# A mixture-of-experts stage whose record loads come in a fixed set per expert instead of one by one

## The reference, cut to what matters

```python
e_flat = expert.reshape(n_assign)            # 2048 tokens x top 2 = 4096 assignments, 32 experts
order = jnp.argsort(e_flat)
tok_sorted = order // TOP_K
...
def expert_block(args):
    xb, e = args
    return (jax.nn.silu(xb @ exp_w1[e]) * (xb @ exp_w3[e])) @ exp_w2[e]
...
y = y_buf.reshape(n_blocks * MOE_BLOCK, d)[dest] * gate_sorted[:, None]
out = jnp.zeros((n_tok, d), h.dtype).at[tok_sorted].add(y)
x = x + g2 * out
```

## Time and profile before

| | us |
|---|---|
| median of 3 runs | 2413.15 |
| the profiled execution, its own time | 2409.21 |
| its span, first to last instruction | 2407.5 |
| expert stage, within the span | about 1596 to 2406 |
| busy in the whole span: PE, DVE, ACT, POOL | 2227.6, 1430.2, 1181.7, 500.8 |
| mean granted TensorE clock | 0.970 |
| bytes moved by the hardware queue q1 | 354.24 MB, 44.6% of 16 engines' span |

### The profile page before, as it was taken

The page is one execution under the profiler, slowest core; times in us unless marked ns, Lnnn a source line. Parts: engine busy times, 40 slices in busy tenths (PEclk is TensorE's granted clock), DMA queues, the critical chain, the costliest instruction groups (busy, mean ns, idle before and its releaser), DMA issues. The chain is left out here.

```text
span 2407.5 us, 43378 instructions
## 1 busy us (share of the span) xinstructions
PE 2227.6 (93%) x15189; PEld 1549.2 (64%) x15190; DVE 1430.2 (59%) x2488; ACT 1181.7 (49%) x2106; POOL 500.8 (21%) x772
## 2 busy tenths in 40 slices
PE   5998999999979999789999999968899999999998
PEld 2335777888856666456666666746666776666775
DVE  4456686232325555555555555466677887666886
ACT  4556322222134444355555555345566666555674
POOL 2662111000001101001222222341222122222122
PEclk8999999999989999899999999979999999999999
DMA  8895222122374543522222221359897988887994
GB/s 303 279 272 139 62 53 79 56 85 62 78 207 98 124 100 89 171 54 80 73 74 71 62 80 58 130 181 330 299 317 254 371 308 290 287 257 252 325 330 145
DMA packets 242118, 414.31 MB, mean 172 GB/s; under 512 B 25601, under 2 KB 129365, under 8 KB 236915
## 3 DMA queue, kind: packets, MB, share of 16 engines
q1 hardware_dynamic: 198048, 354.24, 44.6%
q0 software_dynamic: 18800, 44.94, 7.6%
q10 hardware_dynamic: 25125, 13.18, 2.0%
HBM read 344.83 MB, written 76.85 MB: 175 GB/s over the span
## 5 line engine op out<-in xcount | busy, mean ns | idle before, releaser
L937 PE MATMUL ps_proj<-sb_hTh,sb_winh 128*128 128x512 f32 x576 | 234.4, 407 | 5.2 <-DVE sb_hTl L1089 2.5
L938 PE MATMUL ps_proj<-sb_hTl,sb_winh 128*128 128x512 f32 x576 | 226.5, 393 | 0.0
L939 PE MATMUL ps_proj<-sb_hTh,sb_winl 128*128 128x512 f32 x576 | 224.9, 390 | 0.0
L2258 DVE CUSTOM_DVE_ANT_0 sb_lead<-ps_S,sb_mask 128x640 f32<-128x640 f32 x124 | 102.0, 823 | 87.8 <-PE ps_S L1987 82.0
L2141 ACT ACTIVATE sb_lead<-sb_lead,sb_nm 128x640 f32<-128x640 f32 x128 | 106.3, 830 | 79.2 <-DVE sb_nm L2262 77.6
L1062 ACT COPY sb_rope_or_conv<-ps_proj 128x512 f32<-128x512 f32 x48 | 28.2, 588 | 222.0 <-PE ps_proj L939 147.7
L937 PEld LDWEIGHTS ps_proj<-sb_hTh,sb_winh 128*128 128x128 f32 x576 | 108.8, 189 | 34.6 <-issue 4.1
L2135 ACT COPY sb_lead<-ps_PT 128x512 f32<-128x512 f32 x160 | 89.4, 580 | 74.3 <-PE ps_PT L1979 74.3
L938 PEld LDWEIGHTS ps_proj<-sb_hTl,sb_winh 128*128 128x128 f32 x576 | 108.7, 189 | 25.9 <-issue 4.1
L939 PEld LDWEIGHTS ps_proj<-sb_hTh,sb_winl 128*128 128x128 f32 x576 | 108.5, 188 | 24.2
L2770 POOL DMA_INDIRECT out<-sb_by,sb_rows_out x32 | 69.7, 2177 | 254.1 <-issue 240.1
(11 more groups left out here) (355 smaller groups left out, 5530.0 us busy)
## 6 DMA issues: line engine op xcount, KB each, us to landing
sb_lead<-in_exp_w SPq DMA_DIRECT2D x32, 2048.0 KB, 14.6
sb_w<-in_exp_w SPq DMA_DIRECT2D x32, 2048.0 KB, 9.1
sb_raw<-in_exp_w SPq DMA_DIRECT2D x32, 2048.0 KB, 14.7
sb_ada<-in_ada_w SPq DMA_DIRECT2D x16, 1536.0 KB, 7.7
scr_filt<-sb_fout SPq DMA_DIRECT2D x128, 128.0 KB, 3.1
sb_yh<-scr_filt SPq DMA_DIRECT2D x64, 256.0 KB, 4.9
scr_hy_in<-sb_hcT ACTq DMA_DIRECT2D x12, 1024.0 KB, 5.5
sb_win<-in_w_in SPq DMA_DIRECT2D x9, 1024.0 KB, 6.0
```

The costliest lines, as they stand in the source:

```text
L937: pe.matmul(mp[:, r % 4, 0:N], a, high[:, k, :], start=(k == 0), stop=False)
L938: pe.matmul(mp[:, r % 4, 0:N], a, low[:, k, :], start=False, stop=False)
L939: ins = pe.matmul(mp[:, r % 4, 0:N], b, high[:, k, :], start=False, stop=(k == KT - 1))
L2258: ve.tensor_tensor_reduce(out=pr[:, p, :], in0=mixer_scores if nx.n == 0 and p % 2 else scores_of[p % 2], in1=mask[:, edge, mask_of[p % 2] ...
```

## The change

SP no longer loads records one tile at a time with a wait between them. `records(ex)` waits once, for all batches before it, then loads the main tile's records of `ex` and four lots of `ex + 1`, whether that expert has four, fewer or none. Four lots are four DMAs, one for each group of 32 partitions, of 4 slots each. Slots that were filled too many are written again by later loads. A loop behind `sp.If(many > 5)` loads further lots. `rl` now grows by 80 for each expert, so POOL's `gather` no longer waits for the records of its own tile, but, called from the body of expert `ex`, for the whole batch of `ex + 2` (main tile of `ex + 2` and lots of `ex + 3`); the first one, `gather(1, 1)`, waits for the batches of the experts 0 and 1. The two empty slots at the end become four, loaded with the last batch.

```diff
-            def gather(n):
-                pool.wait_ge(rl, 16 * (n + 2))
+            def records_through(ex):
+                if isinstance(ex, int):
+                    ex = min(ex, NE - 1)
+                return 16 * ((GR + 1) * (ex + 2))
+
+            def gather(n, ex):
+                pool.wait_ge(rl, records_through(ex))
                 pool.wait_ge(tt, n)
...
             def main(n, ex, par, half, last, lots):
-                gather(n + 2)
+                gather(n + 2, ex + 2)
...
-            gather(1)
+            gather(1, 1)
...
-            def records(ex, many, lots):
-                with sp.If(many > 1):
-                    with sp.Fori(0, many - 1) as b:
-                        sp.wait_ge(rl, 16 * (lots + ex + b + 1))
-                        lot = g.table[bass.ds(ex * CAP + P + b * LOT, LOT), :].unsqueeze(0).broadcast_to([GR, LOT, 2])
-                        sp.dma_start(rec[:, bass.ds(lots + ex + b, 1), :].rearrange("p a b -> p (a b)"), lot).then_inc(rl, 16)
-                sp.wait_ge(rl, 16 * (lots + ex + many))
-                sp.dma_start(rec[:, bass.ds(lots + ex + many - 1, 1), :], g.table[bass.ds(ex * CAP, P), :].unsqueeze(1))\
-                  .then_inc(rl, 16)
...
+            def four_lots(ex, slot, b, sem):
+                rows = g.table[bass.ds(ex * CAP + P + b * LOT, 4 * LOT), :].rearrange("(b r) c -> r b c", b=4)
+                for q in range(GR):
+                    sp.dma_start(rec[q * LOT:(q + 1) * LOT, bass.ds(slot + b, 4), :], rows).then_inc(sem, 16)
+
+            def lot_records(ex, many, lots):
+                slot = lots + ex if not isinstance(ex, int) or ex else 1
+                with sp.If(many > 5):
+                    with sp.Fori(4, many - 1, 4) as b:
+                        four_lots(ex, slot, b, rl_more)
+                        sp.wait_ge(rl_more, 16 * GR)
+                        sp.sem_clear(rl_more)
+                four_lots(ex, slot, 0, rl)
+
+            def main_record(ex, many, lots):
+                slot = lots + ex + many - 1 if not isinstance(ex, int) or ex else 0
+                sp.dma_start(rec[:, bass.ds(slot, 1), :], g.table[bass.ds(ex * CAP, P), :].unsqueeze(1)).then_inc(rl, 16)
...
+            def records(ex, total=None):
+                sp.wait_ge(rl, 16 * ((GR + 1) * (ex + 1)))
+                sp.sem_inc(passed_s, 1)
+                main_record(ex, *span(sp, ex))
+                if total is None:
+                    lot_records(ex + 1, *span(sp, ex + 1))
+                else:
+                    for k in range(GR):
+                        nothing(total + k)
...
-            first_records(*first)
-            records(1, *second)
-            records(2, *third)
+            lot_records(0, *first)
+            records(0)
+            records(1)
+            records(2)
...
                 if more:
-                    records(ex + 3, *span(sp, ex + 3))
+                    records(ex + 3, total)
```

More of the change, by code:

```diff
@@ L2505, in stage6 @@
         rl = e.sem("s6_records_loaded")
+        rl_more = e.sem("s6_further_lot_records_loaded")
         gat = e.sem("s6_rows_gathered")
@@ L2801, in first_records @@
[L2801 to L2808, removed]
@@ L2810, in _ @@
-            first, second, third = span(sp, 0), span(sp, 1), span(sp, 2)
+            def four_lots(ex, slot, b, sem):
[10 more added lines that the diff above has]
+                four_lots(ex, slot, 0, rl)
@@ new lines, in main_record, with nothing @@
+            def main_record(ex, many, lots):
+                slot = lots + ex + many - 1 if not isinstance(ex, int) or ex else 0
+                sp.dma_start(rec[:, bass.ds(slot, 1), :], g.table[bass.ds(ex * CAP, P), :].unsqueeze(1)).then_inc(rl, 16)
+            def nothing(slot):
+                sp.dma_start(rec[:, bass.ds(slot, 1), :], g.table[NE * CAP:NE * CAP + P, :].unsqueeze(1)).then_inc(rl, 16)
+            def records(ex, total=None):
[7 more added lines that the diff above has]
+                        nothing(total + k)
@@ L2811, in _ @@
+            first = span(sp, 0)
             sp.wait_ge(blank, 1)
@@ L2815, in _, with next_weights @@
             sp.sem_inc(lhm, 1)
-            first_records(*first)
-            records(1, *second)
-            records(2, *third)
+            lot_records(0, *first)
+            records(0)
+            records(1)
+            records(2)
             sp.wait_ge(g.second_w2, 16)
             sp.sem_inc(ldw2[1], 16)
-            def next_weights(ex, par, lots_last=False, more=True):
+            def next_weights(ex, par, lots_last=False, more=True, total=None):
                 many, lots = span(sp, ex)
@@ L2841, in _ @@
                 next_weights(2 * pair + 1, 1)
-            next_weights(NE - 4, 0)
+            total = sp.value_load(info[0:1, 2, NE - 1:NE], min_val=0, max_val=TILES - NE) + NE
+            next_weights(NE - 4, 0, total=total)
             next_weights(NE - 3, 1, more=False)
[L2845 to L2848, removed]
         @block.tensor
```

## The result

| | before | after |
|---|---|---|
| median of 13 runs, us | 2413.99 (2408.49 to 2419.87) | 2422.53 (2416.87 to 2432.29) |
| span of the profiled execution, us | 2407.5 | 2424.5 |
| mean granted TensorE clock | 0.970 | 0.965 |

The changed kernel is slower: ratio 1.0038, 95% interval 1.0025 to 1.0051, which is 8.5 us between the medians. The forecast was 13.3 us. The two profiled executions lie 17.0 us apart, because the one of before is 4.8 us under its kernel's median and the one of after 3.7 us above. Of the 17.0 us, 3.6 were there when the expert stage began: that shift comes at about 1000 us, in code that is the same in both. Within the stage the profiles differ by 13.5 us.

A forecast was written before the change was run, and what follows sets the result against it. PE sets the pace, with transfers nearly filling the same time. Start 14.5, late weights -1.8, expert 19 -3.4 and expert 5 +4 sum to 13.3 us slower: 2426.5 us against the median of 2413.15, range 2415 to 2439.

The forecast's parts named there:

- The start, 14.5 us: Before the loop: POOL's first gather waits for three batches, PE stalls 12.5 us plus 2 of slow clock (10.5 to 19).
- a sum 3 us lower: At the start: if new lot loads land as fast as the main tile's, the stall would be some 3 us shorter.
- The second gather was covered: At the start: `gather(2)` comes 6.3 to 8.6 us later, but PE needs it only later still, so no cost.
- Late weights at expert 4, -1.8: In the loop: PE's 1.76 us wait at 1711.22 for late weights goes, -1.8 us (0 to -1.8).
- Expert 19, -3.4: Between its lots: weights load before the lots begin, 1.8 us less waiting and 1.6 less slow clock (0 to -4).
- Expert 5, +4: Between its lots: the gather waits for expert 7's records behind weights, PE waits about 7 us, not 3.28 (-3 to +8).
- The added loads, 0: In the loop: four more record loads per expert, 0.25 to 1.25 us each expert, taken as 0 us.
- The 1 us per expert that was taken to be free: In experts without lots: the DMA engines have 5% of 19.3 us free, which would hold the added loads.
- `w2` is not late: On SP: another span and four loads end by 1865, before `w2` followed at 1866.16, so it is not delayed.
- the transfers become the bound: Rival, in runs of experts without lots: weights come late, up to 10 us more, 2436 us; chance 14%.
- the 1.29 us of before: At 1823.39, between two lots: PE waited 1.29 us for a gather, read as a wait with no weights moving.
- 0.06 us of the engines: Each small record load: 0.1 to 0.3 busy in five slices of 62.5 ns, so 0.06 us of the engines.

The follow-up runs named there:

- p3: The kernel before with only the change's start: three batches of five loads that the first two gathers wait for, old loop; 1.0036 of before.
- p1: The changed kernel with the old start, single record loads for experts 0 to 2 on their own semaphore, and the new loop; 1.0002 of before.
- p2: p1, but a gather called from a lot waits for the batch of the next expert, not the one after it; 1.0006 of before.
- e6: p1, but the four lot loads are made only for experts that have lots; 0.9973 of before, 2406.24 us.
- e9: e6 with p2's edit, so a gather in a lot waits for one batch less; 0.9985 of before, 2409.55 us.
- f1: The kernel before plus four lot loads per expert, from expert 3 on, into a spare tile that nothing reads; 1.0053 of before.
- e2: The changed kernel, with the first two gathers waiting for 160 and 240 in place of 240 and 320; 1.0032 of before.
- d1: The changed kernel, with the eight numbers of experts 0 to 3 loaded ahead of the first record load; 1.0027 of before.
- d3: The changed kernel with the edits of d1 and e2 together; 1.0003 of before.
- e7: p1, but experts without lots make their four small loads with a quarter of the elements; 0.9993 of before.
- e5: p1 with eight lot loads per expert in place of four, the added ones into a tile that nothing reads; 1.0017 of before.
- c1: The changed kernel, start and loop, but lot loads are made only for experts that have lots; 0.9999 of before.

## Why the prediction was right, and where it was not

**The time and the sign: right.** Predicted 2426.5 with a range of 2415 to 2439, measured 2422.53. The terms one by one:

- *The start, 14.5 us: the mechanism right, the size too large.* The three landings in a row, the numbers between them, POOL's copy released by a record load and a stall at the turning of the first lot are all in the rows. A batch took 6.3 us, the low end of the 6.3 to 8.6: four loads are issued in 1.75 us, near the short end of what was reckoned. So the copy came 15.7 us after the first load, the low end too, and the stall was 9.2 us, not 12.5; with the slow clock 11.2. The prediction also named a sum 3 us lower, for lot loads that land sooner than the old ones; the stall is 3.3 us shorter than the middle, but no run separates the landing from the issue. p3 against before, and p1 against the changed kernel, give 0.36% or 8.7 us in medians. The second gather was covered, as said.
- *Late weights at expert 4, -1.8: measured -1.7.*
- *Expert 19, -3.4: measured -3.6* (0.64 and 0.57 us of waiting in its lots).
- *Expert 5, +4: measured +2.5*, a wait of 5.03 us in place of about 7. The reason given, the wait for a later batch, is in the changed kernel's row: POOL's copy stood 3.19 us for record loads where it stood 0.45 us for PE before. It is not the whole: in p2 that wait is gone, the gather itself takes longer and PE waits 4.88 us; in p1, with the same loop, PE waits 3.19 us. So +2.5 is the price in one execution, not a fixed one.
- *The added loads, 0: wrong.* This is the step that failed: "four are 0.25 to 1.25 us per expert ... I take 0". 16 of the 29 experts from expert 3 on have no lots, and leaving their loads out won 7 us (p1 1.0002 to e6 0.9973), or 4 by e9: 0.26 to 0.44 us per expert, on the path, near the low bound. f1 shows 13 us for 29 experts in the old loop, 0.45 each. The 1 us per expert that was taken to be free did not cover them. The same part says that `w2` is not late; at 2330.32 it was, by about 1.5 us. The rival *the transfers become the bound* described this and named the right places, late weights at the end of a run of experts without lots: expert 30 lost 1.4 us in the changed kernel's profile, 0.5 in that of p1 and 4 to 6.5 us in those of p2, e2, d1 and d3. It expected the cost as a sum on top; by e6 and e9 it took away a gain of the freed SP that the prediction had counted in only two places, experts 4 and 19.
- *Not foreseen: expert 3 (+2.2) and expert 8 (+2.3).* At expert 8 PE's turning came 7.67 us behind POOL's copy in place of 6.94, and the slow clock that followed cost 1.6 us more. The prediction read the 1.29 us of before as a wait with no weights moving; the view of DMA transfers has q1 moving 0.71 MB from the copy to the turning, and 0.90 MB now. That these 0.2 MB more made the gather later is argued. At expert 3 every engine enters the loop's code for the first time, and PE stands for nothing that the profile names, in before as well. These are one row of before, and one of p1:

```profile
1677.38 0.50 PE L2900 MATMUL ps_bh<-sb_w1h,sb_bxh 128*128 128x512 f32 x1 [2.55 <-issue]
```

```profile
1678.29 0.50 PE L2942 MATMUL ps_bh<-sb_w1h,sb_bxh 128*128 128x512 f32 x1 [3.46 <-issue]
```

The stretch from 1670 to 1682, by the view of DMA transfers, has 326 GB/s moved in before and 368 in p1, both with instruction queues among them. A wait 0.9 us longer was followed by the slow clock. That PE stands there for its instructions, and that they came later because of the freed SP's traffic, is argued, and two rows speak against the second: p3, with the old loop, waits 3.15 us there and loses 3.3, while e7, with the new loop, waits 2.54 and loses nothing. The step at expert 3 is not shown to belong to the change.

So 13.3 against 13.5 us within the stage of the two profiles flatters the working: a start too large by 3.3 us and an expert 5 too large by 1.5 stand against 5.9 us at experts 3, 8 and 30 that were taken as nothing. Between the medians it is 8.5 us. The profiled execution of before lay 4.8 us under its kernel's median, and the same kernel differs from one execution to the next by more (2403.7 to 2422.5 in 35 runs of before in one set), and in the changed loop the late weights come and go: that 13.3 us came out within 0.2 us of the profiles' difference is luck. Where the typical run of before loses what its profile doesn't show was not found.

## What to carry to other kernels

A change that takes waits away from a loader must be read at the point where the pipeline is not yet filled: there a longer fixed set of loads, in batches that wait for one another, is a chain of landings on the path, and the loads that the first consumer needs should be issued first and waited for alone. In a stage where PE and the transfers both stand near their limits, a load is not free because it is small: count the small packets beside the bulk loads and the loader's time for issuing them, and issue none whose data nobody reads. Here the best version keeps the batch and the old start and skips the loads of experts without lots: 0.9973 of the time before (0.9963 to 0.9984). It is the best of twelve kernels, and e9, which differs in one wait, gave 0.9985, so the gain over the kernel before is 4 to 7 us and not surely 7.

## What the runs showed of the hardware that I had not expected

- A small packet (under 512 B) beside the bulk loads took about 11 ns of one DMA engine, an estimate from q1's share of the whole stage in e6, p1 and e5 above. I had read 0.06 us of the engines for a load of 128 packets, 7 ns a packet. The 16 GB/s between e6 and p1 in the first stretch would give 27 ns if all of it were the packets'; the other stretches and the whole stage do not bear that out.
- Behind an empty queue the landing of the last of four small loads held SP only 1.5 us: in d1 their issue ended at 1604.15 + 1.75 = 1605.90 and the next batch began at 1607.42. Before, counted alike from the end of the issue, one load held it 1.65 and 2.36 us.
- PE's slow clock comes behind the idle, not at once. After 2.55 us (d3) the turnings behind it still took 0.66 and 0.60 us, as without a wait, and the output product 1.10 in place of 0.73; the granted clock of 1616 to 1617 is 1.00 there, of 1618 to 1620 it is 0.50, the lower level, 1.2 GHz. After 1.99 us (expert 8) it was the same: turnings of 0.66 us, then an output product of 3.50 in place of 1.93. After 4.17 us and more (d1 at expert 5, p2, c1, the changed kernel) the turnings themselves took 1.11 or 1.12 us. After 1.29 us before nothing was slow.
